# A two-layer mixer and a mixture-of-experts stack on one core: normalisation sums and gate matmuls set among other matmuls

## What is computed

```
first_block:   layer 0: x += gate * (concat(conv(h), rwkv7(h)) @ even_w_out)
               layer 1: h = rms_norm(x) * g * (1 + scale) + shift
                        q, k, v, qi, ki, wi, g = split(h @ odd_w_in)
                        score = sum_h wi * relu(rope(qi) . rope(ki));  keep the top 64 keys of each query
                        o = softmax(rope(q) . rope(k), kept keys) @ v           16 heads of 128, one key head
                        x += gate * ((o * silu(g)) @ odd_w_out)
               return rms_norm(x) * final_g
second_block:  h = x;  hn = rms_norm(h) * ln_mix[0]
               h += concat(diff_attention(hn), short_conv(hn)) @ a_w_out
               h += swiglu(rms_norm(h));  h += sigmoid(rms_norm(h) @ ple_gate) * (p @ ple_proj)
               h += spatial_gating(layer_norm(gelu(rms_norm(h) @ c_w_in))) @ c_w_out
               h += moe_swiglu(rms_norm(h), 8 experts, top 2);  the same ple step again
               return rms_norm(h) * final_norm
```

## Time and profile before

| | |
|---|---|
| median of 3 runs | 2431.33 us (2429.09 to 2434.85) |
| the profiled execution's own time | 2434.66 us |
| its span, first to last instruction | 2432.8 us |
| PE, PEld, DVE, ACT busy | 2132.0, 1879.7, 1381.9, 811.3 us |
| mean granted clock of TensorE | 0.919 of full speed |
| layer 1 attention (`attend(0, ...)`), 718.6 to 816.9 | 98 us |
| the mixture of experts, 1526 to 2346 | 820 us |

### The profile page before, as it was taken

How to read it: one execution, slowest core, us unless ns; L and a number is a source line. 1 busy time by engine, 2 the same in 40 slices (tenths; PEclk the granted TensorE clock), 3 DMA queues, 4 the chain that set the end, 5 groups by cost and what they waited for, 6 DMA issues and landing times.

```text
span 2432.8 us, 28820 instructions
## 1 busy us (share of the span) xinstructions
PE 2132.0 (88%) x12163; PEld 1879.7 (77%) x12163; DVE 1381.9 (57%) x1637; ACT 811.3 (33%) x881; POOL 32.8 (1%) x74
## 2 busy tenths in 40 slices
PE   5997998869986879568988877999999999999977
PEld 4777887656854767458987666989999998999966
DVE  6688766324033211438761112788787888878851
ACT  2411121111112110211101111667676676766641
POOL 2000000000000000000000000000000000000000
PEclk8998999888995889688999998999999999999988
DMA  8736213212430123114664313699899998999950
GB/s 287 253 121 203 75 36 139 70 69 84 159 104 0 66 75 138 35 35 139 187 176 150 127 35 120 248 340 349 323 355 328 334 351 322 356 326 339 350 211 18
DMA packets 225573, 452.13 MB, mean 186 GB/s; under 512 B 6929, under 2 KB 91161, under 8 KB 225449
## 3 DMA queue, kind: packets, MB, share of 16 engines
q1 hardware_dynamic: 222128, 445.44, 52.2%
q0 software_dynamic: 1632, 4.75, 0.7%
q10 hardware_dynamic: 1688, 0.15, 0.1%
HBM read 448.21 MB, written 2.10 MB: 185 GB/s over the span
## 4 chain that ended last, share of the span: by engine, by line
PE 85%; DVE 11%; ACT 2%; issue 1%; DMA 0%; ACTq 0%; DVEq 0%; POOL 0%
PE bank L812 20%; PE bank L1543 20%; PE bank L838 10%; PE bank L1726 9%; PE bank L550 8%; PE bank L1569 3%; PE bank L783 1%; PE bank L790 1%; PE bank L640 1%; PE bank L653 1%; DVE arena L2415 1%; DVE hT L2241 1%; PE bank L823 1%; ACT arena L2018 1%; DVE nr L2239 1%
## 5 line engine op out<-in xcount | busy, mean ns | idle before, releaser
L1381 DVE TENSOR_TENSOR ring_r<-ring,his_r 128x2816 fp32r<-128x2816 f32 (+1 forms) x192 | 587.1, 3086 | 61.1 <-ACT his_r L1030 60.8
L1030 ACT ACTIVATE his_r<-ring 128x2816 fp32r<-128x2816 f32 (+1 forms) x192 | 491.2, 2561 | 198.1 <-DMA ring<-in_moe_w_dram 185.5
L812 PE MATMUL bank<-his_r,hg_r 128*128 128x352 f32 x2048 | 355.5, 325 | 0.8 <-ACT hg_r L1041 0.8
L1543 PE MATMUL bank<-hT,ring 128*128 128x256 f32 x1424 | 323.4, 391 | 29.5 <-DVE hT L2241 22.4
L1543 PEld LDWEIGHTS bank<-hT,ring 128*128 128x128 f32 x1424 | 279.5, 197 | 73.6 <-DVE hT L2241 24.0
L812 PEld LDWEIGHTS bank<-his_r,hg_r 128*128 128x128 f32 x2048 | 332.9, 188 | 2.0 <-issue 0.9
L1726 PE MATMUL bank<-hT,ring 128*128 128x256 f32 x912 | 216.0, 394 | 14.4 <-DVE arena L2261 10.8
L1726 PEld LDWEIGHTS bank<-hT,ring 128*128 128x128 f32 x912 | 175.5, 196 | 43.1 <-issue 18.3
L812 PE MATMUL bank<-ring_r,hg_r 128*128 128x352 f32 x1024 | 186.1, 324 | 0.0
L812 PEld LDWEIGHTS bank<-ring_r,hg_r 128*128 128x128 f32 x1024 | 169.3, 188 | 0.0
L1543 PE MATMUL bank<-arena,ring 128*128 128x256 f32 x672 | 149.8, 386 | 16.8 <-DVE arena L1242 9.7
(11 more groups left out here) (423 smaller groups left out, 2333.5 us busy)
## 6 DMA issues: line engine op xcount, KB each, us to landing
ring<-in_moe_w_dram SPq DMA_DIRECT2D x128, 1408.0 KB, 8.4
ring<-in_moe_w_dram SPq DMA_DIRECT2D x48, 1536.0 KB, 9.1
ring<-in_even_w_in_dram SPq DMA_DIRECT2D x28, 1024.0 KB, 6.8
ring<-in_ada_w_dram SPq DMA_DIRECT2D x24, 1024.0 KB, 8.8
ring<-in_ffn_w_dram SPq DMA_DIRECT2D x22, 1024.0 KB, 5.3
ring<-in_odd_w_in_dram SPq DMA_DIRECT2D x9, 2048.0 KB, 7.7
ring<-in_moe_w_dram SPq DMA_DIRECT2D x16, 1024.0 KB, 7.1
ring<-in_a_w_in_dram SPq DMA_DIRECT2D x6, 2048.0 KB, 8.1
```

The lines of the kernel that those rows point to most:

```text
L812: ins = mm(bank[first + m][:, 0:WC], x[:, KT // 2 * late + k, :], w[:, k, WC * m:WC * m + WC], start=(not late and k == 0 and s == "hg_hi" ...
L1030: A(moe_hi(n), moe_w(n), ACT.Copy).then_inc(sem("moe_hi"), 1)
L1381: V.tensor_tensor(moe_lo(n), moe_w(n), moe_hi(n).bitcast(F32), ALU.subtract).then_inc(sem("moe_lo"), 1)
L1543: mm = nc.tensor.matmul(bank[q % 4][0:width, 0:T], w[:, k, m * P:m * P + width], rhs(k), start=(k == 0), stop=(k == ph["k"] - 1))
```

## The change

Five rearrangements; the arithmetic stays, but for one normalisation that is worked out from sums in another form.

1. **Sums behind the tiles.** ACT squares one tile of `xT` when that tile has been updated (`square`), and PE makes the ones-matmul of tile q - 2 right after the phase's tile q (`norm_tile`, `norm_behind`), in bank 4; the last three stand after the last tile. So for the norms after `eoB`, `ao`, `f2`, `pp0`, `cout` and `pp1`. The next phase waits for each tile of `hT` by itself (`h_waits`). Before a root ACT runs one Sqrt on a single column (`root`). In `ple` the addition to `xT` is made tile by tile.
2. **Two norms in one pass.** After `oo` ACT makes both the squares and the squares times final_g; PE sums both behind the tiles (`norm_pair`, banks 4 and 5); DVE gets the second norm's sum from the second row of sums and the first root, writes `hT` first, and rescales `xT` in the next phase.
3. **Angles and sines moved.** `dve_angles` stands ahead of DVE's eight takes of `eoB`; ACT's sines stand behind norm 1.
4. **Beside `q`.** Rotations 0 to 3 stand after the first two tiles of `q`, and two index products after each of tiles 3 to 10; `q` uses banks 0 and 1. Four gate tiles stand between the rotations 4 to 11, in pairs.
5. **Gates inside the attention.** The other 12 gate tiles stand in steps 0 to 11, in bank 3: four matmuls after the logits, ahead of the wait for the weights, and four after the transposes. ACT takes a gate tile with a plain copy and applies Silu to four tiles at once after every fourth; DVE's product with the result waits for `gates_ready` at every fourth step.

The transposes of `p_2` (`embed`) also move from behind `f2` to ahead of it. The diff, cut to its core:

```diff
-            norm(1, [took("eoB", 8)])
...
-            pe_gemm("m1", h, [(sem("h_ready"), KT * 2)], special={1: values})
-            pe_gemm("m2", h, [took("m1", 4)], special={2: index_keys, 3: head_weights})
-            pe.wait_ge(*took("m2", 4))
-            rot(0, 4)
-            pe.wait_ge(sem("rot_done"), 4)
-            for n in range(16):
+            def h_waits(i):
+                return lambda k: (sem("h_ready"), KT * i + k + 1)
+            def index(n):
...
-            pe_gemm("q", h, [])
-            pe_gemm("g", h, [took("q", 16)])
-            rot(4, 12)
-            pe.wait_ge(sem("rot_done"), 12)
-            pe.wait_ge(*took("g", 16))
...
+            def beside_q(q):
+                if q == 0:
+                    pe.wait_ge(*took("m2", 4))
+                    rot(0, 2)
+                elif q == 1:
+                    rot(2, 4)
+                elif 3 <= q < 11:
+                    index(2 * (q - 3))
+                    index(2 * (q - 3) + 1)
+            pe_gemm("m1", h, [], special={1: values}, ready=h_waits(1))
+            pe_gemm("m2", h, [took("m1", 4)], special={2: index_keys, 3: head_weights})
+            pe_gemm("q", h, [took("m2", 4)], between=beside_q, banks=2)
+            def gate_half(q, half):
+                w = wait_chunk(pe, "g", q // 4, 0)
+                if half == 0:
+                    if q == 0:
+                        pe.wait_ge(*took("m2", 4))
+                    else:
+                        pe.wait_ge(*took("g", q))
+                for k in range(KT // 2 * half, KT // 2 * (half + 1)):
+                    ins = mm(bank[3][:, 0:T], w[:, k, (q % 4) * P:(q % 4 + 1) * P], h(k), start=(k == 0), stop=(k == KT - 1))
+                if half == 1:
+                    ins.then_inc(acc_ready, 1)
+            def gate_tile(q):
+                gate_half(q, 0)
+                gate_half(q, 1)
+            gate_tile(0)
+            for i in range(3):
+                pe.wait_ge(*took("q", 4 * i + 4))
+                rot(4 + 2 * i, 6 + 2 * i)
+                gate_tile(i + 1)
+            pe.wait_ge(*took("q", 16))
...
+                        fill(b, 0)
...
+                        fill(b, 1)
...
-            attend(0, 16, 2, logits, turned, result)
-            pe_gemm("oo", lambda k: GT[:, k, :], [(sem("o_taken"), 16)])
-            norm(2, [took("oo", 8)])
-            norm(3, [])
+            pe.wait_ge(sem("rot_done"), 12)
+            attend(0, 16, 2, logits, turned, result, lambda b, half: gate_half(4 + b, half) if b < 12 else None)
+            def norm_pair(q):
+                if q >= 2:
+                    norm_tile(2, q - 2)
+                    norm_tile3(q - 2)
+                if q == KT - 1:
+                    for p in (KT - 2, KT - 1):
+                        norm_tile(2, p)
+                        norm_tile3(p)
+            def norm_tile3(q):
+                pe.wait_ge(sem("norm_scaled"), q + 1)
+                ins = mm(bank[5][:, 0:T], ones[:, :], SQ3[:, q, :], start=(q == 0), stop=(q == KT - 1))
+                if q == KT - 1:
+                    ins.then_inc(sem("pair_summed"), 1)
+            pe_gemm("oo", lambda k: GT[:, k, :], [(sem("o_taken"), 16)], between=norm_pair)
...
-            pe_gemm("qk", h, [(sem("h_ready"), KT * 4)])
+            pe_gemm("qk", h, [], ready=h_waits(2))
...
-            pe_gemm("ao", lambda k: OD[:, k, :] if k < 4 else CV[:, k - 4, :], [(sem("o_normed"), 1)])
-            norm(4, [took("ao", 8)])
+            pe_gemm("ao", lambda k: OD[:, k, :] if k < 4 else CV[:, k - 4, :], [(sem("o_normed"), 1)], between=norm_behind(3))
...
+                if j < KT - 1:
+                    norm_behind(4)(j)
...
+            def ple(i, nrm):
+                pe_gemm(f"pg{i}", h, [], ready=h_waits(nrm))
+                pe_gemm(f"pp{i}", lambda k: PPT[2 * i + k], [took(f"pg{i}", 8), (sem("toks_taken"), TK_P + 2)], between=norm_behind(nrm + 1))
...
+            norm(1, lambda q: took("eoB", q + 1))
+            shifted(1)
             act.wait_ge(sem("angles_ready"), 1)
             for k in range(3):
                 A(ROT[:, k, 1, :], ANG[:, k, :], ACT.Sin, scale=small[:, 11 + k:12 + k]).then_inc(sem("rot_tables"), 1)
             A(ROT[:, :, 0, :], ANG2[:, :, :], ACT.Sin).then_inc(sem("rot_tables"), 1)
-            norm(1, [took("eoB", 8)])
-            shifted(1)
...
-            take_gemm(act, "q", lambda q, lin, b: A(QT[:, q, :], b, ACT.Copy))
-            take_gemm(act, "g", lambda q, lin, b: A(GT[:, q, :], b, ACT.Silu))
...
+            def gate_tile(q):
+                act.wait_ge(acc_ready, phases["g"]["t0"] + q + 1)
+                A(GT[:, q, :], bank[3][:, 0:T], ACT.Copy).then_inc(acc_taken["act"], 1)
+                if q % 4 == 3:
+                    act.wait_ge(*took("g", q + 1))
+                    A(GT[:, q - 3:q + 1, :], GT[:, q - 3:q + 1, :], ACT.Silu).then_inc(sem("gates_ready"), 1)
...
+                    fill(b)
+            attend(0, 16, 2, 6, 2 * T, lambda b: gate_tile(4 + b) if b < 12 else None)
...
+            for q in range(KT):
+                act.wait_ge(*took("oo", q + 1))
+                square(2, q)
+                A(SQ3[:, q, :], xT[:, q, :], ACT.Square, scale=col("final_g", q)).then_inc(sem("norm_scaled"), 1)
+            root(2)
...
+            act.wait_ge(sem("norm_scaled"), KT + 1)
+            A(segm[:, :], segm[:, :], ACT.Sqrt, bias=1e-6, scale=1.0 / D).then_inc(sem("pair_rooted"), 1)
...
+                if b % 4 == 0:
+                    dve.wait_ge(sem("gates_ready"), b // 4 + 1)
...
-            norm(2, lambda ct: col("final_g", ct), dst=xT)
+            dve.wait_ge(sem("norm_rooted"), 3)
+            step(V.reciprocal(nr[:, :], nr[:, :]))
+            dve.wait_ge(sem("pair_summed"), 1)
+            step(V.tensor_tensor(segm[:, :], bank[5][:, 0:T], nr[:, :], ALU.mult))
+            V.tensor_tensor(segm[:, :], segm[:, :], nr[:, :], ALU.mult).then_inc(sem("norm_scaled"), 1)
+            ch(V.tensor_tensor(gs[:, 0:8], cols8("final_g"), cols8("mix0"), ALU.mult))
+            dve.wait_ge(sem("pair_rooted"), 1)
+            step(V.reciprocal(segm[:, :], segm[:, :]))
+            step(V.tensor_tensor(segm[:, :], segm[:, :], nr[:, :], ALU.mult))
+            for ct in range(KT):
+                V.scalar_tensor_tensor(hT[:, ct, :], xT[:, ct, :], gs[:, ct:ct + 1], segm[:, :], ALU.mult, ALU.mult).then_inc(sem("h_ready"), 1)
             dve.wait_ge(sem("h_ready"), KT * 3)
-            norm(3, lambda ct: col("mix0", ct))
+            for ct in range(KT):
+                V.scalar_tensor_tensor(xT[:, ct, :], xT[:, ct, :], col("final_g", ct), nr[:, :], ALU.mult, ALU.mult).then_inc(sem("x_normed"), 1)
...
+                def add(q):
+                    dve.wait_ge(*took(f"pp{i}", q + 1))
+                    V.tensor_tensor(xT[:, q, :], xT[:, q, :], PG[:, q, :], ALU.add).then_inc(sem("embedded"), 1)
+                take_gemm(dve, f"pp{i}", lambda q, lin, b: V.tensor_tensor(PG[:, q, :], PG[:, q, :], b, ALU.mult),
+                          between=lambda q: add(q - 1) if q else None)
+                add(KT - 1)
...
+        def norm_tile(i, q):
+            nc.tensor.wait_ge(sem("norm_squares"), KT * i + q + 1)
+            ins = nc.tensor.matmul(bank[4][:, 0:T], ones[:, :], NSQ[i][:, q, :], start=(q == 0), stop=(q == KT - 1))
+            if q == KT - 1:
+                ins.then_inc(sem("norm_summed"), 1)
+        def norm_behind(i):
+            def f(q):
+                if q >= 2:
+                    norm_tile(i, q - 2)
+                if q == KT - 1:
+                    norm_tile(i, KT - 2)
+                    norm_tile(i, KT - 1)
+            return f
...
+            def square(i, q):
+                A(NSQ[i][:, q, :], xT[:, q, :], ACT.Square).then_inc(sem("norm_squares"), 1)
+            def norm(i, ready):
+                for q in range(KT):
+                    act.wait_ge(*ready(q))
+                    square(i, q)
+                root(i)
+            def root(i):
+                if i >= 1:
+                    A(small[:, 62:63], ones[:, 0:1], ACT.Sqrt)
...
+            dve_angles(dve, V, ch, step)
             for q in range(KT):
                 out("eoB", q, bank[q % 4][:, 0:T])
-            dve_angles(dve, V, ch, step)
```

More of the change, by code:

```diff
@@ L952, in act_rest, with beside_q, attend @@
                 A(RELU[:, n % 2, :], bank[7 if n % 2 == 0 else 4][:, 0:T], ACT.Relu, scale=HD ** -0.5).then_inc(sem("relu_done"), 1)
-            take_gemm(act, "q", lambda q, lin, b: A(QT[:, q, :], b, ACT.Copy))
-            take_gemm(act, "g", lambda q, lin, b: A(GT[:, q, :], b, ACT.Silu))
-            def attend(n0, count, ahead, banks, width):
+            def beside_q(q):
+                if 3 <= q < 11:
+                    index(2 * (q - 3))
+                    index(2 * (q - 3) + 1)
+            take_gemm(act, "q", lambda q, lin, b: A(QT[:, q, :], b, ACT.Copy), banks=2, between=beside_q)
+            def gate_tile(q):
[4 more added lines that the diff above has]
```

(40 more changed lines are left out.)

104 lines of the change are left out of this document (51 added, 53 removed).

## The result

The changed kernel takes 2311.78 us, the median of 4 runs (2307.22 to 2314.36), against 2431.74 of the kernel before (2429.09 to 2434.85, 4 runs): ratio 0.9504, 95% interval 0.9485 to 0.9523. The forecast was 2308. The profiled execution after is the fastest of its four, 4.6 us under the median, so that the spans of the two profiles (2432.8 and 2305.1) lie 127.7 us apart and the medians 120.0.

A forecast was written before the change was run, and what follows sets the result against it. PE work was 85% of the span, with time to gain where PE waits or its clock is low. Norms 60.0, `m2` to logits 62.7 and attention 0.4 gave 123.1 us off 2434.66: 2308 median, range 2290 to 2342.

The forecast's parts named there:

- behind `eoB`: Gap between `eoB` and `m1`: 7.7 us in place of 24.75, 17.0 saved.
- behind `oo`: Gap of two norms between `oo` and `qk`: 14.4 us in place of 26.82, 12.4 saved.
- `m2` to the first logits: Layer 1 ahead of the attention: 89.0 us in place of 151.7, 62.7 saved, 41.6 of it gate tiles only moved.
- the attention: Layer 1: 98.0 us in place of 98.4 with 12 gate tiles inside, a filled step 6.56 us at the high clock.
- the 1.0 that I had charged for a slow start of `qk`: After `oo`: PE stands still 9 us and `qk` starts at the low clock, so 1.0 us was added to the gap.
- Rival 2: Filled attention: the clock stays low, a step takes 11.5 us, 59 us lost, 2367 us; chance 8%.
- Rival 1: Attention: the first half of each gate tile is not hidden under DVE's wait, 21 us lost, 2329 us; chance 12%.
- Rival 3: Norms: squares come late, PE waits inside the phases, and the 60 us shrink to a third, 2348 us; chance 5%.
- Rival 4: From `q` to the attention's end: interleaving keeps the clock low, 136 us more, 2444 us, slower than before; chance 2%.
- the 2.17 us of the five early ones-matmuls: Norms: five of eight ones-matmuls stand ahead of the phase's last tile, which makes it 2.17 us longer.
- some 8 us from the last gemm record to `m1`'s first: Sign in the changed kernel's profile: after `eoB`, some 8 us pass before `m1`'s first record.
- the attention's order: Filled step: four gate matmuls (1.74 us) lie under DVE's 2.36, the second four add 1.74; PE idles 0.6 of 6.56 us.

The follow-up runs named there:

- the gates outside: The change with all 12 gate tiles of the attention moved ahead of it, behind the last rotations: 2360.23 us, ratio 0.9705 to the kernel before.
- the sums at the end: The change with all ones-matmuls of a norm made behind the phase's last tile: 2302.47 us, ratio 0.9465 to the kernel before.
- the other two: The change with whole gate tiles ahead of the transposes and all ones-matmuls behind each phase's last tile: 2291.47 us, ratio 0.9424 to the kernel before.

## Why the prediction was right

By its own steps, each stage from its first PE record to the next stage's, profile against profile (before less after; predicted in brackets):

- behind `eoB` 16.9 (17.0); behind `oo` 13.3 (12.4); `ao` 2.3 (2.8); `f2` 8.6 (8.1); `pp0` 7.9 (7.8); `cout` 2.6 (2.8); behind the experts 2.9 (2.8); `pp1` 5.6 (6.3). Together 60.1 (60.0).
- `m2` to the first logits: 151.7 to 88.9, 62.8 (62.7).
- the attention: 98.4 to 96.6, 1.7 (0.4); the step is 6.48 (6.56), the clock 1.00, as forecast.
- not foreseen: `m1` and `m2` 1.4 and `cin` to `cout` 1.1 shorter, the router 2.7 longer. That these three come to nothing together is luck. Code ahead of `eoB` that is the same took 3.3 less in this profile; over all runs here `eoB` starts anywhere from 475.0 to 478.3, so this is scatter. The experts, from their first matmul to PE's last ahead of the norm: 817.5 both times.

The sum is 127.7, the predicted 123.1; against the medians, 120.0. That the total was 3.8 us off is within what one execution differs from another, and each predicted term of a stage was right to 1.3. The 0.9 more than forecast behind `oo` are the 1.0 that I had charged for a slow start of `qk`: that phase takes 29.4 us after and 29.3 before, so its low clock was in both kernels and should not have been charged.

Point by point. The heart of it, that a full step at the high clock lasts as long as an empty one at the low clock, is shown by the gates outside (attention 96.1, step 6.90, clock 0.57) beside the change (96.6, filled step 6.48, clock 1.00). Rival 2 was false for the change, but not far off: with the whole tile behind the transposes the clock did fall in part. Rival 1, the uncovered half tile, was false: 1.73 of DVE's 2.35 are covered. Rival 3 was false as it was put; PE does not wait inside the phases of 3.47-us tiles. In the ple phases its concern was half right: in `pp0` PE waits 0.43 us ahead of the first sum, and three of the sums take 0.70 in place of 0.43, and the sums at the end gain 2.9 and 2.7 us in the two ple steps. Rival 4 was false: in the stretch 551 to 606, index products and all, PE is busy 55.00 of 55.00 us at 1.00.

One step is charged correctly and yet has its sense wrong: the 2.17 us of the five early ones-matmuls were taken as the price of a gain, and the sums at the end show that the early place is a plain loss of 8 us. The sign by which to know this stage was also put wrongly: "some 8 us from the last gemm record to `m1`'s first" counts these 2.17 us, which lie ahead of that record. By the same sum the gap should be 5.5, and it is 5.73. The other step is the attention's order: I worked out that 0.6 us of DVE stays uncovered, while the second half of each tile is paid in full, and did not ask what it would be worth to move that half ahead too: 10.3 us.

The Trainium skill (ScalarE: Activation LUTs, "What ACT_TABLE_LOAD costs") puts a switch at about 2.66 us. The traces agree on the load, 1.28, but show no drain: the Sqrt behind it starts 0.01 later, and in the Silu step above each instruction follows its load, and each load the instruction before it, within 0.02. A further 1.4 us a norm would have shown as a gap near 7.1 behind `eoB` where 5.73 stands. On the clock the traces agree in direction with the Trainium skill (TensorE: Matmul & The Clock Gate, "HAM oscillation — how this bites in real kernels"), which says that idle gaps between matmuls send the clock back; its example is a loop with longer waits, for DMA. With gaps of 2.4 us a step the clock was 0.57 in the empty attention, with 0.6 it was 1.00. The gap alone doesn't settle it: with the same 2.4 us and the whole tile behind the transposes it was 0.86.

## What to carry to other kernels

Where PE's clock is low because each step waits for another engine, independent matmuls can be put into the step nearly free, as long as the higher clock pays for them. Put them into the wait until it is covered (here 2.6 us for 2.35), because the wait that stays bare is paid on top. Work that PE must do anyway gained nothing here by being moved between busy tiles; behind the last tile it hid the last tile's take, square and table load. Before moving an instruction off the path, look for what releases the same wait next: the load of 1.28 was worth only 0.5 to 0.6 a norm.

## What the hardware showed that I had not expected

PE kept busy in the gaps of the norms with matmuls without a reader is worth 9.4 us alone and 10.6 on top of the other two, and it is a loop of two lines and its calls. `qk` and `pg0` behind their gaps lost 1.8 and 1.7 us to the low clock, and a list of small matmuls behind one lost more, 3.2 us in 32 router products and 1.7 in the 16 transposes ahead of them.

Why the router's products ran at 0.90 of the clock in the kernel before and at 0.50 in the change stays open: PE stands still for 5.5 us ahead of the transposes in both, and with the sums at the end, hence dense as before, they take 6.64 us too, as they do in every experiment but the two with added matmuls. With the gap filled they run at 1.00.
